# Block-diagonal recurrent state, and a tail interleaved by token tile, in a two-block transformer kernel

## The reference

```
def step(state, inp):                       # one token after the other
    sa = einsum('bhvk,bhk->bhv', state, -kk_t)
    state = state * w_t + sa[..., None] * b_t + v_t[..., None] * k_t
    return state, einsum('bhvk,bhk->bhv', state, r_t)
o = (o - mean(o)) * rsqrt(var(o) + GN_EPS) * ln_w + ln_b     # per head
o = (o + bonus) * g
y_rwkv = o @ w_rwkv_out                                      # 512 -> 1024
mixed = gates[..., :D] * y_att + gates[..., D:] * y_rwkv
x = x + mixed @ w_out                                        # 1024 -> 1024
x = x + hierarchical_moe(rms_norm(x))       # routes each token to 2 of 32 experts
```

## Time and profile before

| what | value |
|---|---|
| median of 3 runs | 1620.84 us (1619.93 to 1621.74) |
| the profiled execution | 1619.48 us, of which span 1617.7 us |
| mean granted clock of PE | 0.964 |
| PE busy | 1523.5 us, 94% |
| VectorE, ScalarE, GpSimd busy | 43%, 34%, 27% |
| mean DMA rate over the span | 217 GB/s |

### The profile page before, as it was taken

The page is one execution under the profiler, slowest core; times in us unless marked ns, Lnnn a source line. Parts: engine busy times, 40 slices in busy tenths (PEclk is TensorE's granted clock), DMA queues, the critical chain, the costliest instruction groups (busy, mean ns, idle before and its releaser), DMA issues.

```text
span 1617.7 us, 21837 instructions
## 1 busy us (share of the span) xinstructions
PE 1523.5 (94%) x8374; PEld 1109.8 (69%) x8374; DVE 694.5 (43%) x1077; ACT 544.7 (34%) x820; POOL 443.9 (27%) x159
## 2 busy tenths in 40 slices
PE   7989999999899999999889899998999999999997
PEld 6778999987788999987657589854544354444443
DVE  3775556545863755561438255423211112112121
ACT  5546533445555533444345321102011011011010
POOL 4362434442643343447957021000000000000000
PEclk9999999999989999999989999798999999999999
DMA  6341455554232555567544310015699999999993
GB/s 242 125 150 53 135 205 180 184 179 167 99 105 79 167 198 186 179 199 225 209 133 161 123 57 1 1 52 208 254 428 428 428 428 428 428 428 428 428 428 162
DMA packets 44400, 351.77 MB, mean 217 GB/s; under 512 B 5171, under 2 KB 7135, under 8 KB 19743
## 3 DMA queue, kind: packets, MB, share of 16 engines
q1 hardware_dynamic: 43630, 349.37, 56.4%
q10 hardware_dynamic: 576, 1.13, 0.2%
q0 software_dynamic: 112, 0.17, 0.1%
HBM read 347.71 MB, written 1.07 MB: 216 GB/s over the span
## 4 chain that ended last, share of the span: by engine, by line
PE 62%; DMA 17%; DVE 8%; issue 6%; ACT 2%; DVEq 2%; POOL 1%; SPq 0%; POOLq 0%; ACTq 0%
DMA ring<-in_w_expert_up 16%; PE psum L994 12%; PE psum L996 12%; PE psum L995 12%; PE psum L1587 9%; PE psum L983 3%; PE psum L1613 2%; PE psum L1553 1%; PE psum L1062 1%; PE psum L1446 1%; DVE arena L2083 1%; DVE arena L2126 1%; PE psum L1081 1%; PE psum L964 1%; DVEq L2158 1%
## 5 line engine op out<-in xcount | busy, mean ns | idle before, releaser
L872 POOL TENSOR_TENSOR weights_split<-weights_raw,weights_split 128x2048 fp32r<-128x2048 f32 (+4 forms) x108 | 390.1, 3625 | 426.3 <-ACT weights_split L1682 426.1
L1682 ACT ACTIVATE weights_split<-weights_raw 128x2048 fp32r<-128x2048 f32 (+4 forms) x154 | 243.4, 1585 | 284.9 <-PE psum L996 284.7
L1587 PE MATMUL psum<-ring,arena 128*64 128x512 f32 x1024 | 234.1, 612 | 19.6 <-DMA ring<-in_w_expert_up 18.5
L1587 PEld LDWEIGHTS psum<-ring,arena 128*64 128x64 f32 x1024 | 75.3, 140 | 175.2 <-issue 175.2
L994 PE MATMUL psum<-weights_split,h_split 128*128 128x512 f32 (+3 forms) x400 | 155.4, 388 | 16.6 <-DVE arena L2360 6.4
L995 PE MATMUL psum<-weights_split,h_split 128*128 128x512 f32 (+3 forms) x400 | 153.3, 383 | 0.0
L996 PE MATMUL psum<-weights_split,h_split 128*128 128x512 f32 (+3 forms) x400 | 153.1, 383 | 0.0
L994 PE MATMUL psum<-weights_split,hidden_split 128*128 128x512 f32 (+1 forms) x384 | 151.0, 393 | 1.5 <-DVE hidden_split L1670 1.5
L995 PE MATMUL psum<-weights_split,hidden_split 128*128 128x512 f32 (+1 forms) x384 | 149.1, 388 | 0.0
L996 PE MATMUL psum<-weights_split,hidden_split 128*128 128x512 f32 (+1 forms) x384 | 149.0, 388 | 0.0
L994 PE MATMUL psum<-h_split,weights_split 128*128 128x256 f32 x512 | 145.2, 284 | 1.3 <-DVE weights_split L872 1.3
(11 more groups left out here) (367 smaller groups left out, 2155.2 us busy)
## 6 DMA issues: line engine op xcount, KB each, us to landing
weights_raw<-in_layer_w SPq DMA_DIRECT2D x94, 1024.0 KB, 4.8
ring<-in_w_expert_gate SPq DMA_DIRECT2D x32, 2048.0 KB, 16.2
ring<-in_w_expert_up SPq DMA_DIRECT2D x32, 2048.0 KB, 17.1
arena<-in_w_expert_down SPq DMA_DIRECT2D x32, 2048.0 KB, 13.4
weights_raw<-in_second_w SPq DMA_DIRECT2D x44, 512.0 KB, 4.3
weights_raw<-in_layer_w SPq DMA_DIRECT2D x6, 768.0 KB, 4.1
ring<-in_w_out SPq DMA_DIRECT2D x2, 2048.0 KB, 17.0
ring<-in_w_rwkv_out SPq DMA_DIRECT2D x1, 2048.0 KB, 9.7
```

Of the source, the lines that this page charges most:

```text
L872: eng.tensor_tensor(W.part(j, 1, n), W.raw(j, n), W.part(j, 0, n).bitcast(F32), ALU.subtract).then_inc(W.lo[W.pieces[j][1]], 1)
L1587: ins = pe.matmul(bank[half(j), :], xe[h][:, k, half(j)], w[j][:, k, :], start=(k == 0), stop=(k == KD - 1))
L1682: act.activation(W.part(j, 0, w), W.raw(j, w), ACT.Copy).then_inc(W.hi, 1)
```

## The change

The state is kept as 128 x 128 for each pair of heads: the two 64 x 64 blocks stand on the diagonal and GpSimd zeroes the rest once. A product with it is then one matmul of 128 rows and 128 columns for a pair, where there were two of 64 rows and 64 columns. RHS, U and OUT are now units by half of the pairs instead of by parity; RHS waits for the last level of both parities. The tail is done by token tile: the first tile's `oT` and `yrw` stand between the core steps of the second tile, and the other units of both tiles follow in an order written out by hand, in which the second tile's `head_norm` runs beside products of the first. The bridge matmuls are gone. `hTr` and `oT` lie elsewhere in SBUF. SyncE asks for the first turn's matrices in the order 0, 1, 4, 5, 2, 3, and places 4 and 5 wait for the last `yrw`.

```
-        plan += [("RHS", 2 * t + par, 4 * par, "A") for par in range(2)]
-        plan += [("U", 2 * t + par, 4 * par + 1, "A") for par in range(2)]
-        plan += [("OUT", 2 * t + par, 4 * par + 2, "V") for par in range(2)]
+        plan += [("RHS", 2 * t + i, 4 * i, "A") for i in range(2)]
+        plan += [("oT", 0, 3, "A")] if t else []
+        plan += [("U", 2 * t + i, 4 * i + 1, "A") for i in range(2)]
+        plan += [("yrw", 0, 7, "V")] if t else []
+        plan += [("OUT", 2 * t + i, 4 * i + 2, "V") for i in range(2)]
...
-    plan += interleave("oT", 2, (0, 1), "A")
-    plan += interleave("yrw", 2 * T, (2, 3, 4, 5), "V")
-    plan += interleave("mixT", 4, (6, 7, 0, 1), "A")
-    wout, turned_x = interleave("wout", 2 * T, (2, 3, 4, 5), "V"), interleave("tr2", 4, (6, 7, 0, 1), "AV")
-    plan += wout[:3] + turned_x[:2] + wout[3:] + turned_x[2:]
-    plan += interleave("route", T, (2, 3), "V")
+    plan += [("mixT", 0, 3, "A"), ("yrw", 1, 0, "V"), ("mixT", 1, 4, "A"), ("wout", 0, 1, "V"), ("oT", 1, 3, "A"), ("wout", 1, 5, "V"),
+             ("yrw", 2, 7, "V"), ("yrw", 3, 0, "V"), ("tr2", 0, 6, "V"), ("mixT", 2, 2, "A"), ("tr2", 1, 3, "V"), ("mixT", 3, 4, "A"),
+             ("route", 0, 1, "V"), ("wout", 2, 7, "V"), ("tr2", 2, 5, "V"), ("wout", 3, 0, "V"), ("tr2", 3, 6, "V"), ("route", 1, 2, "V")]
...
             # SyncE
-            for dst, src, s in matrices(0):
-
-                units.wait_full(SW.last[s] if s < SLOTS else ("oT", 1))
+            first_turn = list(matrices(0))
+            for s in (0, 1, 4, 5, 2, 3):
+                units.wait_full(SW.last[s] if s < SLOTS else ("yrw", 2 * T - 1))
+                dst, src, _ = first_turn[s]
...
             # TensorE, the core
-                    for c in range(PAIRS):
-                        o = bank[:, c * RW_E:(c + 1) * RW_E]
-                        ins = pe.matmul(o, m["Mak"][:, c, :], value(c, par), start=True, stop=(t == 0))
+                units.wait_emptied(*((m, 2 * t + par) for m in ("Mak", "Mrb", "Mrk") for par in range(2)),
+                                   *(("XT", 8 * (2 * t + par) + len(LEVELS) - 1) for par in range(2)))
+                for i in range(2):
+                    bank = units.begin(("RHS", 2 * t + i))
+                    for c in (2 * i, 2 * i + 1):
+                        o = bank[:, c % 2 * P:(c % 2 + 1) * P]
                         if t:
-                            ins = pe.matmul(o, rwT[0][r, c, tok], minus_state[r, c, :], start=False, stop=True)
+                            pe.matmul(o, rwT[0][:, c, tok], minus_state[:, c, :], start=True, stop=False)
+                        for par in range(2):
+                            ins = pe.matmul(o[:, par * RW_E:(par + 1) * RW_E], core[par]["Mak"][:, c, :], value(c, par),
+                                            start=(t == 0), stop=(t == 0 or par == 1))
+                    units.finish(("RHS", 2 * t + i), ins)
+                if t:
+                    pe.wait_ge(o_ready, 1)
+                    row_transposes(pe, units, ("oT", 0), bufA[:, 0, :])
...
+                if t:
+                    units.wait_emptied(("oT", 0))
+                    project_rw(0)
...
-            bridge(pe, units, ("oT", 0), 18)
...
-            bridge(pe, units, ("mixT", 0), 6)
...
             # TensorE, the tail
+            mix_rows(0, 0)
+            project_rw(1)
+            project_out2(0, 0, low)
+            mix_rows(0, 1)
+            project_out2(0, 1, low)
+            project_out2(0, 0, high)
+            pe.wait_ge(o_ready, 2)
+            row_transposes(pe, units, ("oT", 1), bufA[:, 1, :])
+            project_out2(0, 1, high)
+            units.wait_emptied(("oT", 1))
+            project_rw(2)
+            project_rw(3)
+            turn_rows(0, 0)
+            mix_rows(1, 0)
+            turn_rows(0, 1)
+            project_out2(1, 0, low)
+            mix_rows(1, 1)
+            project_out2(1, 1, low)
             pe.wait_ge(route_loaded, 48)
+            route(0, 0)
+            route(0, 1)
+            project_out2(1, 0, high)
+            project_out2(1, 1, range(4, 6))
+            turn_rows(1, 0)
+            project_out2(1, 1, range(6, KD))
+            route(1, 0)
+            turn_rows(1, 1)
+            route(1, 1)
...
             # VectorE
+            def gate_rw(u):
+                t, c = u // 2, u % 2
+                bank = units.wait_full(("yrw", u))
+                g, a = gates[:, t, D + c * 512:D + (c + 1) * 512], gates[:, t, c * 512:(c + 1) * 512]
+                units.emptied_by(("yrw", u), dve.tensor_tensor(g, bank, g, mul), "V")
+                dve.drain()
+                dve.tensor_tensor(a, a, g, add).then_inc(mixed, 1)
...
+                if t:
+                    dve.sem_inc(o_ready, 1)
+                    gate_rw(0)
...
-            for step in range(len(LEVELS)):
+            for step in range(3):
+                head_norm(1, step)
+            gate_rw(1)
+            for step in range(3, len(LEVELS)):
                 head_norm(1, step)
             dve.sem_inc(o_ready, 1)
...
+            add_out2(0)
+            add_out2(1)
+            dve.wait_ge(route_loaded, 48)
+            gate_rw(2)
+            gate_rw(3)
+            turned(0)
+            turned(1)
+            inverse_root(0)
+            empty_route(0)
+            add_out2(2)
+            turned(2)
+            add_out2(3)
+            turned(3)
+            inverse_root(1)
+            empty_route(1)
```

More of the change, by code:

```diff
@@ L975, in transposes, with row_transposes @@
                 units.finish((stage, j), ins)
+        def row_transposes(pe, units, key, src):
+            bank = units.begin(key)
+            for k in range(src.shape[1] // P):
+                ins = pe.transpose(bank[:, k * P:(k + 1) * P], src[:, k * P:(k + 1) * P], ident)
+            units.finish(key, ins)
         def token_major(pe, units, key, lhs, w, ks=None):
@@ new lines, in _ @@
+                if t:
+                    pe.wait_ge(o_ready, 1)
+                    row_transposes(pe, units, ("oT", 0), bufA[:, 0, :])
+                for i in range(2):
+                    units.wait_emptied(("RHS", 2 * t + i))
+                    bank = units.begin(("U", 2 * t + i))
+                    for h in range(4 * i, 4 * i + 4):
+                        ins = pe.matmul(bank[:, h % 4 * RW_E:(h % 4 + 1) * RW_E], core[h % 2]["TT"][:, h // 2, :],
+                                        rhs[:, h // 2, h % 2 * RW_E:(h % 2 + 1) * RW_E], start=True, stop=True)
+                    units.finish(("U", 2 * t + i), ins)
@@ new lines, in _ @@
+                if t:
+                    units.wait_emptied(("oT", 0))
+                    project_rw(0)
+                for i in range(2):
+                    units.wait_emptied(("U", 2 * t + i))
+                    bank = units.begin(("OUT", 2 * t + i))
+                    for c in (2 * i, 2 * i + 1):
+                        o = bank[:, c % 2 * P:(c % 2 + 1) * P]
+                        if t:
+                            pe.matmul(o, rwT[3][:, c, tok], state[:, c, :], start=True, stop=False)
+                        for par in range(2):
+                            o_h = o[:, par * RW_E:(par + 1) * RW_E]
+                            pe.matmul(o_h, core[par]["Mrb"][:, c, :], rw_u[:, 2 * c + par, :], start=(t == 0), stop=False)
+                            ins = pe.matmul(o_h, core[par]["Mrk"][:, c, :], value(c, par), start=False, stop=(t == 0 or par == 1))
+                    units.finish(("OUT", 2 * t + i), ins)
@@ L1525, in _, with mix_rows, project_out2 @@
-            route(range(4))
-            units.wait_emptied(("wout", 2), ("wout", 3))
-            transposes(pe, units, "tr2", x, (2, 3))
-            units.wait_emptied(("tr2", 2), ("tr2", 3))
-            route(range(4, KD))
+            def mix_rows(t, c):
+                pe.wait_ge(mixed, 2 * t + c + 1)
+                row_transposes(pe, units, ("mixT", 2 * t + c), gates[:, t, c * 512:(c + 1) * 512])
+            def project_out2(t, c, ks):
+                if ks[0] % 4 == 0:
+                    units.wait_emptied(("mixT", 2 * t + ks[0] // 4))
+                token_major(pe, units, ("wout", 2 * t + c), lambda k: hT[:, k, t * P:(t + 1) * P], weights(("out", c)), ks)
@@ new lines, in turn_rows, with route @@
+            def turn_rows(t, c):
+                units.wait_emptied(("wout", 2 * t + c))
+                row_transposes(pe, units, ("tr2", 2 * t + c), x[:, t, c * 512:(c + 1) * 512])
+            def route(t, c):
+                units.wait_emptied(("tr2", 2 * t + c))
+                token_major(pe, units, ("route", t), lambda k: hTr[:, k, t * P:(t + 1) * P], w_route, range(4 * c, 4 * c + 4))
+            low, high = range(4), range(4, KD)
+            mix_rows(0, 0)
+            project_rw(1)
@@ L2065, in _ @@
                                ALU.mult).then_inc(bonus_v, 1)
+            pool.memset(state, 0.0)
             pool.memset(zeros, 0.0)
```

146 lines of the change are left out of this document (48 added, 98 removed).

## The result

The changed kernel took 1595.26 us, the median of 4 runs (1589.97 to 1598.6); the kernel before took 1621.29 us beside it (4 runs). The ratio is 0.9833, 95% interval 0.981 to 0.9856: 26 us faster. The forecast was 1592.6 within 1587 to 1602.5. The profiled execution took 1589.97 us with a span of 1588.1 us, against a forecast span of 1589.5.

A forecast was written before the change was run, and what follows sets the result against it. PE's order from the second tile's level loop on was taken to set the end; 29.3 us gained, less 1.0 and 0.13, gave 28.2, so 1620.84 - 28.2 = 1592.6 us, range 1587 to 1602.5.

The forecast's parts named there:

- The core: Second tile's RHS, U and OUT on PE: 8.96 us if the clock holds, instead of 23.46 us.
- rival C: In the core, the wide product stays dear at 0.18 us a record: +4.5 us, 1597; chance 0.05.
- The waits: Ahead of RHS, waiting for both parities' last add: RHS 0.8 us later in tile 1, 1.0 in tile 0.
- the sum: First routing reduce 29.3 us earlier, less 1.0 and 0.13: 28.2 us gained, forecast 1592.6 us.
- The list laid end to end: PE's order from second tile's RHS at 1030.3 to the last wout, full near 1087.1 instead of 1113.4.
- the terms of 1.0 and 0.13: Delays ahead of tile 1: tile 0's RHS wait, 1.0 us, and the wider negated state on VectorE, +0.13 us.
- rival B: Handovers between engines in PE's list cost time: ten entries at 0.8 us, +8, 1600.6; chance 0.11.
- The fillers: Matmuls ahead of oT and mixT that compute nothing: removal costs nothing, the 7.8 us of norm they covered going under products.
- rival A: The clock still falls in a thin place of the core: +6.5 us, 1599; chance 0.14.
- the routing stretch: VectorE's chain from its first reduce to the first expert matmul: 19.06 us, kept by the changed kernel.
- The loads: First turn's expert matrices: downs over by 1084, ups by 1097, read about 7 us behind 1111, 20 us of cover.
- rival E: At the expert loop, late weight loads hide the gain and the span stays: about 1620; chance 0.01.

The follow-up runs named there:

- run 2: The kernel before with only the block-diagonal state and units by half of the pairs, old tail and filler matmuls kept: 1607.03 us, ratio 0.9911.
- run 3: The changed kernel with RHS, U and OUT by parity again, 64-row state products alternating with 128-row ones, new tail kept: 1608.52 us, ratio 0.9905.
- run 5: The changed kernel with the wait on both parities' last level moved from ahead of RHS to ahead of U: 1588.15 us, ratio 0.9804.
- run 4: The kernel before without its 24 filler matmuls and nothing else changed: 1621.99 us, ratio 0.9996.
- run 8: The changed kernel with 64-row state products again, grouped ahead of the 128-row ones, row halves in turn, each parity in its own bank: 1598.23 us.
- run 6: The changed kernel with four 512-column filler matmuls between the rank products and the gather: 1592.31 us, ratio 0.9836.
- run 7: The changed kernel with 21 filler matmuls of 256 columns in TensorE's three waits at the end of the second block's attention: 1592.47 us, ratio 0.9837.
- run 10: The changed kernel with SyncE asking for the first turn's matrices in the old order, 0 to 5: 1591.85 us, ratio 0.9823.
- run 1: The changed kernel again with no edit, for a second profile: 1596.23 us, ratio 0.9835.
- run 11: The changed kernel with later wait ahead of U, filler matmuls ahead of the gather and near the end of the attention: 1591.18 us, ratio 0.9803.
- run 9: The changed kernel with the wait moved ahead of U and four filler matmuls ahead of the gather: 1585.85 us, ratio 0.9786.

## Why the prediction was right, and what it had wrong

**The core, predicted 8.96 us, measured 8.87.** Term by term: RHS 2.70 and 2.73, U 1.80 and 1.73, OUT 4.46 and 4.41. The product with 128 columns to which 64-column ones are added costs no more than others (rival C): in OUT 0.27 us for its pair and 0.18 for the next, 0.110 a record over OUT's 40 records (4.41 us). That the core and the tail are two separate gains, runs 2 and 3 show (16.0 and 14.8).

**The waits.** Both RHS idle times are 0.78 us; together they cost 1.84 us by run 5, against 1.8 in the sum. The negated state takes 0.43 us, against 0.29 + 0.13.

**The list laid end to end.** It was laid from an RHS at 1030.3; the real one started at 1031.92, 1.62 later (1.13 of it are the terms of 1.0 and 0.13 that the sum takes off at its end). Shifted by 1.62, the list has oT1 at 1059.4 (measured 1059.35), wout2 low behind its 0.4 us stall at 1071.9 (1071.81, behind 0.25) and the last `wout` over at 1088.3 (1088.31). The list's own end is 1086.7 with the stall in it; the prediction then goes on from 1087.1, which counts the 0.4 us a second time. Without that slip the sum is 28.6 us. Handovers between engines cost nothing even where the other engine is done only 1.2 us ahead (oT0 starts at 1034.65, the norm's last step ends at 1033.42); rival B is out. From the end of the last `wout` to the reduce it took 3.86 us, against 3.7. The core stretch was to be 60.5 us (1090.8 - 1030.3) and is 60.25. From the first product of the core to the reduce the kernel gains 30.4 - 1.7 = 28.7 us.

**The fillers** were to cost nothing to remove; in the changed order that held, and run 4 shows why it isn't a rule: without products in their place the removal costs 1.4 us. The prediction also took them to fill no more than the wait for the norm; at half clock they ran 1.8 us beyond it.

**The clock** (rival A, 0.14) held in the core in every profile without alternating heights. The case for rival A was that the clock had fallen in thin work, records of 64 columns. Runs 2, 3 and 8 narrow that: in the core it does not fall with 64-column records of one height, nor with 64-row ones in a block; it fell whenever the two heights alternated. The runs don't tell whether the change of height itself counts or the slower pace that it brings, 0.18 us a record.

**The rules weighed.** The rule on products in different row groups (the Trainium skill, TensorE: Matmul & The Clock Gate, Part 3) agrees with run 8: 0.065 us a record. That the old kernel had none of it fits the prediction's reason, that neighbours shared rows; that merging gives nothing up was true only of the old order. Grouped halves come within 0.74 us of the diagonal state in the core stretch. Part 1 of the same page of the Trainium skill ties the fall of the clock to idle time; run 3 disagrees as the kernel before did, with a fall 23 us behind the last idle time. At the gather it fits: 4.39 us idle, then 0.50. But the clock had already been down once there, at 0.59 in the window 1092 to 1096, behind idle times of no more than 0.79 and 0.44 us. Part 4 of the Trainium skill's page says that transposes don't count as activity in the same way; with the groups of four among the products the clock stayed at 1.00 from 1028 to 1088.

**What was off: the routing stretch.** The prediction kept it at 19.06 us; it measured 19.88. Most of the difference is the gather, 6.24 us where the kernel before had:

```profile
1132.48 5.62 PE L1553 MATMUL psum<-arena 128*128 128x128 f32 x32 [4.18 <-DVE arena L2666]
```

At full clock it takes 3.81 us (run 6), so both kernels run most of it at half clock. The term had the right mechanism and a size that isn't fixed: runs 2, 3, 4, 5, 7 and 8 don't touch this code either and have 18.84 to 19.94 us. So the 0.8 us is not shown to be a price of the change. What run 6 shows is that holding the clock is worth 1.4 to 2.5 us here.

**The loads** had 20 us of cover by the sum; in run 10 the last one came 10 us later with no effect, and rival E is out. **The sum** gave 28.2 us; the three stretches give 27.9, the medians 26.0. The profiled spans differ by 29.6 us, run 1's by 23.6; both distances from 27.9 lie in stretches that the change doesn't touch. For the medians no trace says where their 2 us lie, and that the median came within 3 us of 1592.6 is in part luck, since those stretches alone move a span by more.

## What to carry to other kernels

When an in-order engine is always busy, look at what each stretch of its list costs per record and which records compute nothing: filler work marks a wait that useful work of another tile can take. Products on few rows cost most here when they alternate with full-row ones (0.18 us a record); merge them into full rows (0.11) or group them with the row halves in turn (0.065 for twice as many), the two differ by 0.4 us in the core. Put each wait directly ahead of the first instruction that needs the data, and where the clock matters to a short burst behind an idle time, a few dead matmuls can pay.

## What the runs showed of the hardware that was not expected

Two stretches took one of two lengths, though hardly any edit touches them. The first is the end of the attention, which only runs 7 and 11 edited: 62.5 us in five profiles (before, runs 2, 4, 5, 6) and 65.8 in six (the changed kernel, runs 1, 3, 8, 9, 10). The windows show the clock, first the changed kernel's, then run 6's:

```profile
914.00:918.00 4.00, 3.10 (x20) 2.91 (x21) 0.28 (x1) 0.81 (x1) 0.00 (x0) 0.66 0.00 0
918.00:922.00 4.00, 4.00 (x14) 3.01 (x14) 0.28 (x1) 0.00 (x0) 0.00 (x0) 0.50 0.00 0
```
```profile
914.00:918.00 4.00, 3.50 (x23) 2.62 (x22) 1.60 (x5) 1.26 (x4) 0.00 (x0) 1.00 0.00 0
918.00:922.00 4.00, 2.32 (x20) 2.21 (x20) 0.28 (x1) 1.45 (x2) 0.00 (x0) 1.00 0.00 0
922.00:926.00 4.00, 4.00 (x16) 2.46 (x16) 0.28 (x1) 0.00 (x0) 0.00 (x0) 0.68 0.00 0
```

PE is idle there for the same short times in all of them (1.29, 0.90 and 2.92 us), and the clock falls in all of them; what differs is how soon. Where it falls early, the 12 records behind the idle time of 0.90 us take 2.82 us instead of 1.55. The changed kernel and its repeat both have the longer length and the three kernels with the old tail the shorter; but kernels with the new tail have both, ahead of any edited code, so a link with the change is neither shown nor excluded.

The second is first expert matmul to load-out: 471.6 to 472.0 us in five profiles (the changed kernel, runs 1, 4, 9, 10) and 472.9 to 474.0 in the other eight. In the five, PE waits 0.2 to 0.3 us for the last up matrices of the loop; in the eight it waits 1.9 to 2.0 us, and in six of these the clock falls behind that wait, so that 32 records take 8.78 us instead of 7.09. What delays these loads is open.

Such steps, and the 5.9 us of run 1, make a single span uncertain by some 6 us, three times the range of the first three runs of the kernel before (1619.93 to 1621.74).
